# A chunked RWKV recurrence: level products on four quadrants of the array, rows of v from DRAM, outputs summed in PSUM

## The reference

```python
def wkv_scan(s0, r, w, k, v, a, b, reverse):
    def step(s, inp):
        r_t, w_t, k_t, v_t, a_t, b_t = inp
        sa = jnp.einsum('bhvk,bhk->bhv', s, a_t)
        s = s * w_t[:, :, None, :] + sa[..., :, None] * b_t[:, :, None, :] + v_t[..., :, None] * k_t[:, :, None, :]
        return s, jnp.einsum('bhvk,bhk->bhv', s, r_t)
```

## Time and profile before

| | us |
|---|---|
| median of 3 runs | 2601.62 |
| lowest, highest | 2598.08, 2608.76 |
| profiled execution | 2604.29 |
| its span in the profile | 2602.5 |
| TensorE busy in the span | 2314.5 (89%) |
| VectorE busy | 1688.6 (65%) |
| ScalarE busy | 1025.3 (39%) |
| GpSimd busy | 661.3 (25%) |

### The profile page before, as it was taken

How to read it: one execution, slowest core, us unless ns; L and a number is a source line. 1 busy time by engine, 2 the same in 40 slices (tenths; PEclk the granted TensorE clock), 3 DMA queues, 4 the chain that set the end, 5 groups by cost and what they waited for, 6 DMA issues and landing times. The chain is left out here.

```text
span 2602.5 us, 50127 instructions
## 1 busy us (share of the span) xinstructions
PE 2314.5 (89%) x20892; PEld 1847.3 (71%) x20892; DVE 1688.6 (65%) x2155; ACT 1025.3 (39%) x1633; POOL 661.3 (25%) x659
## 2 busy tenths in 40 slices
PE   5998988899999669999777999999973999999993
PEld 2886755568877558888636899997652888888883
DVE  5990559551115445666576776774657999999994
ACT  3112541231014420001154545444132877777773
POOL 1331568123320023222006666650000100000000
PEclk8998999999999779999878999998986999999997
DMA  6232004421104445211053111104142999999994
GB/s 237 96 124 75 1 33 142 132 99 45 49 14 185 151 156 193 96 41 40 14 185 92 32 32 29 29 20 169 57 174 97 409 407 396 396 393 405 396 378 158
DMA packets 136485, 401.77 MB, mean 154 GB/s; under 512 B 56314, under 2 KB 67834, under 8 KB 108754
## 3 DMA queue, kind: packets, MB, share of 16 engines
q1 hardware_dynamic: 124180, 360.02, 37.3%
q0 software_dynamic: 4608, 16.78, 2.7%
q10 hardware_dynamic: 7488, 21.99, 2.2%
HBM read 341.05 MB, written 57.69 MB: 153 GB/s over the span
## 5 line engine op out<-in xcount | busy, mean ns | idle before, releaser
L3900 DVE TENSOR_TENSOR ex_wl<-ew_raw,ex_wh 128x2048 fp32r<-128x2048 f32 x192 | 435.6, 2290 | 41.7 <-ACT ex_wh L3862 38.2
L3862 ACT ACTIVATE ex_wh<-ew_raw 128x2048 fp32r<-128x2048 f32 x192 | 367.6, 1919 | 109.5 <-PE ex_U L3806 40.3
L118 PE MATMUL sp_acc<-b2h_hi,sp_wh 128*128 128x512 f32 (+1 forms) x528 | 194.7, 369 | 16.2 <-POOL sp_wl L1729 16.2
L118 PE MATMUL sp_acc<-b2h_lo,sp_wh 128*128 128x512 f32 (+1 forms) x528 | 194.4, 368 | 0.0
L118 PE MATMUL sp_acc<-b2h_hi,sp_wl 128*128 128x512 f32 (+1 forms) x528 | 194.2, 368 | 0.0
L3783 POOL DMA_INDIRECT x<-ex_o,ex_at x16 | 26.5, 1656 | 490.2 <-DVE ex_o L3923 490.2
L2621 PE MATMUL rc_chain<-rc_x,rc_near 64*64 64x64 f32 x3200 | 132.8, 222 | 5.3 <-DVE rc_near L2503 2.2
L1727 POOL CAST sp_wh<-sp_w 128x1024 fp32r<-128x1024 f32 x26 | 28.3, 1088 | 402.2 <-DMA sp_w<-in_w_conv 221.4
L2621 PEld LDWEIGHTS rc_chain<-rc_x,rc_near 64*64 64x64 f32 x3200 | 111.1, 135 | 19.2 <-issue 9.0
L118 PEld LDWEIGHTS sp_acc<-b2h_hi,sp_wh 128*128 128x128 f32 x528 | 100.1, 190 | 33.9 <-POOL sp_wl L1729 16.6
L118 PEld LDWEIGHTS sp_acc<-b2h_lo,sp_wh 128*128 128x128 f32 x528 | 100.2, 190 | 16.4
(11 more groups left out here) (520 smaller groups left out, 5887.6 us busy)
## 6 DMA issues: line engine op xcount, KB each, us to landing
ew_raw<-in_exp_gate SPq DMA_DIRECT2D x64, 1024.0 KB, 8.0
ew_raw<-in_exp_up SPq DMA_DIRECT2D x64, 1024.0 KB, 9.5
ew_raw<-in_exp_down SPq DMA_DIRECT2D x64, 1024.0 KB, 8.0
b2p_pT<-in_ada_w SPq DMA_DIRECT2D x32, 512.0 KB, 6.0
rc_ac<-ac SPq DMA_DIRECT2D x40, 256.0 KB, 3.4
b_pj<-in_ada_w SPq DMA_DIRECT2D x8, 1024.0 KB, 12.5
ssm_wm<-in_w_merge SPq DMA_DIRECT2D x16, 512.0 KB
ac<-rp_ac SPq DMA_DIRECT2D x4, 2048.0 KB, 7.1
```

The lines of the kernel that those rows point to most:

```text
L118: ins = nc.tensor.matmul(out, w[a][:, k, :], h[b][:, k, cols], start=(first and n == 0), stop=(last and n == 2))
L3862: nc.scalar.activation(wh[:, n % RING], raw[:, n % RING], ACT.Copy).then_inc(q["w_hi"], 1)
L3900: V.tensor_tensor(wl[:, n % RING], raw[:, n % RING], wh[:, n % RING].bitcast(f32), ALU.subtract).then_inc(q["w_lo"], 1)
```

## The change

1. Level products: `diagonal` becomes `chain`. The second pair of blocks (j = 1) writes its result to the other half of the partitions (p ^ j), on the way back `advanced` takes it from there, so that the 8 matmuls go round all four quadrants. `chain` has one region in two banks for both products instead of one bank each.
2. For that, `advanced` needs the transposed matrix of the second pair of blocks in the other half: `moved` on ScalarE copies it into `xo`, two copies of 64 partitions by 128, at each of the five levels. `advanced` and `inverted` wait for `xt_moved`.
3. Rows of v: `rwkv_prepare` transposes v at its start on TensorE, ten tiles of 128 tokens; ScalarE copies them from PSUM (into `wide`, used later), and SP stores them in DRAM. `logits(0)` waits until all ten are copied. In the recurrence `load_v(c)` on SP fetches them straight into `uv` with eight transfers per chunk, after `s_done` and `y_crossed`. `v_staged` and both `v_rows` go.
4. Outputs: `outputs_of_state` goes. `outputs` makes, for each of four regions, four 64x64 matmuls with the state (start) and then four matmuls over 128 partitions (stop) into the same PSUM region; VectorE adds once to `y`.
5. The orders of all engines in the recurrence are written anew. Direction 1 now leads, and the context chunks and others run in a staggered way.

```diff
@@ rwkv_prepare: SP, ScalarE, TensorE
+                for i in range(TILES):
+                    sp.wait_ge(q["v_out"], i + 1)
+                    sp.dma_start(v_dram[i * P:(i + 1) * P, :], v_staged[:, i]).then_inc(q["v_stored"], 16)
...
+                for i in range(TILES):
+                    act.wait_ge(q["v_turned"], i + 1)
+                    nc.scalar.activation(v_staged[:, i], acc[:, i % 6 // 2, i % 2], ACT.Copy).then_inc(q["v_out"], 1)
...
+                for i in range(TILES):
+                    if i >= 6:
+                        pe.wait_ge(q["v_out"], i - 5)
+                    for b in range(HP):
+                        last = nc.tensor.transpose(acc[:, i % 6 // 2, i % 2, b * P:(b + 1) * P], pT[:, VB + b, i * P:(i + 1) * P], T.ident[:])
+                    last.then_inc(q["v_turned"], 1)
...
                     if u == 0:
+                        pe.wait_ge(q["v_out"], TILES)
@@ rwkv_chunks: SP
+                def load_v(c):
+                    for d in range(2):
+                        if c:
+                            sp.wait_ge(joint["s_done"], c)
+                        if c > CTX_CK:
+                            sp.wait_ge(joint["y_crossed"], c - CTX_CK)
+                        for e in range(2):
+                            own = t[d]["uv"][e * CK:(e + 1) * CK].rearrange("p f (j a) t -> p f j a t", a=2)
+                            rows = v_dram[at(c, d):at(c, d) + CK, :].rearrange("r (j a f t) -> r f j a t", a=2, f=2, t=CK)
+                            for f in range(2):
+                                sp.dma_start(own[:, f, :, 1 - e, :], rows[:, f, :, 1 - e, :]).then_inc(q[d]["v_loaded"], 16)
@@ ScalarE
-                        A.activation(t[d]["t1"][:], chained(d, 0), ACT.Copy).then_inc(q[d]["t1_ready"], 1)
+                        A.activation(paired(t[d]["t1"][:]), chained(d), ACT.Copy).then_inc(q[d]["t1_ready"], 1)
+
+                def moved(c, d, l):
+                    if runs(c):
+                        b, s = t[d], q[d]
+                        act.wait_ge(s["xt_next"], LEVELS * c + l + 1)
+                        for p in range(2):
+                            frm, to = slice(p * CK, (p + 1) * CK), slice((1 - p) * CK, (2 - p) * CK)
+                            A.activation(b["xo"][to], b["xt"][frm, 2:4], ACT.Copy).then_inc(s["xt_moved"], 1)
@@ VectorE
-                def outputs_of_state(c, d):
...
-                for k in range(NCK + 1):
+                for k in range(NCK + 2):
+                    advanced(k - 1, 0, 0)
+                    outputs(k - 2, 1)
...
@@ TensorE
-                def diagonal(d, bank, l, r):
...
+                def quarters():
+
+                    for f, j, p in product(range(2), range(HP // 2), range(2)):
+                        yield 2 * j + f, j, f, p, p ^ j
+
+                def chain(d, back, l, r):
+
+                    for h, j, f, p, o in quarters():
+                        frm, to = (o, p) if back else (p, o)
+                        k = slice(frm * CK, (frm + 1) * CK)
+                        last = M(chained(d)[to * CK:(to + 1) * CK, j, f], l(h, p)[k], r[k, h], start=True, stop=True)
...
+                        pe.wait_ge(s["xt_moved"], 2 * (LEVELS * c + l + 1))
+                        chain(d, True, lambda h, p: b["xo"][:, h - 2] if h >= 2 else b["xt"][:, h], b["t1"]).then_inc(s["xp_done"], 1)
...
-                        stacked(lambda b, f, j, e: (b["uv"][:, f, 2 * j + e], b["near"][:, c % 2, f, 1, 2 * j + e])).then_inc(joint["y_crossed"], 1)
...
+                        for j, d in product(range(HP // 2), range(2)):
+                            b, at = t[d], slice((2 * d + j) * CK, (2 * d + j + 1) * CK)
+                            for e, f in product(range(2), range(2)):
+                                k, h = slice(f * CK, (f + 1) * CK), 2 * j + e
+                                M(W[k, e, at], b["S"][k, h], b["ar"][k, c % 2, h, CK:], start=True, stop=False)
+                            for e, f in product(range(2), range(2)):
+                                k, h = slice(f * CK, (f + 1) * CK), 2 * j + e
+                                last = M(W[k, e, at], b["uv"][:, f, h], b["near"][:, c % 2, f, 1, h], start=False, stop=True)
+                        last.then_inc(joint["y_crossed"], 1)
```

272 lines of the change are left out of this document (120 added, 152 removed).

## The result

The changed kernel takes **2632.54 us** (median of 4 runs, 2631.96 to 2635.96); the kernel before took 2599.85 us beside it (2597.32 to 2608.76). The ratio is 1.0123, with a 95% interval of 1.0102 to 1.0143. The forecast was 2595.6 us with a range of 2555 to 2618: the direction was wrong and the range too low. The profiled execution has a span of 2630.3 us, against 2602.5 us before: 27.8 us more.

What follows compares the result with a forecast made beforehand. TensorE was taken to bound the recurrence. Prepare +7.0, context chunks -4.4, the 19.59 us chunk -1.5, 14 full chunks -8.1, last chunk and tail +1.0 gave -6.0 us; off the 2601.62 us median, 2595.6 us, range 2555 to 2618.

Steps and rivals of the forecast that it cites:

- The walk: Path followed through one recurrence chunk, engines strictly in order: 19.2 us against 19.78; 16.5 against 17.98 in context chunks.
- Level products on four quadrants: In the recurrence, 18 products per chunk go from 0.46 to 0.23 us, saving 4.1 us of TensorE per chunk.
- The rival that they don't run at once: Level products stay at 0.46 us in the recurrence: 20.4 us per chunk, 2618 us in all; chance 0.03.
- The outputs' block: On TensorE in the recurrence, 64 pairs with eight shape changes of 0.18 us last 3.2 us.
- `rwkv_prepare`: Phase ahead of the recurrence: first logits wait for ten copies of v and start 7.0 us later.
- The copies across: `moved` on ScalarE in the recurrence: 0.20 us a copy, 0.40 a pair, 0.54 until the product may start.
- the copies across cost more: Rival: a pair of `moved` copies takes 0.67 us, giving 20.3 us per chunk and 2615 us; chance 0.07.
- GpSimd's order has slack in it: In the chunk walk, GpSimd's last scaling of direction 0 is done at 16.6 us, when ScalarE is there too.
- the two lower rivals: TensorE stays close to the bound in the recurrence: 2575 us, or 2538 us if only its own work counts; chance 0.33.
- Rows of v: Loads in the recurrence: eighth issue at 13.4 to 13.9, wanted at 17.5, hidden below 3.6 to 4.1 us of landing.
- the rival of the late rows: Rows of v land late in the recurrence: 2615 us at 4.9 us of landing, 2655 at 7; chance 0.10.
- The clock: In the recurrence, TensorE was read at its full clock, 1.00, the 2.4 GHz level.

Runs made afterwards that it cites:

- e3_grouped: Changed kernel with the outputs' 64 pairs in two groups, first all products with the state, then all with u and v: 2617.84 us.
- e11_copies_twice: Changed kernel with each of the 20 `moved` copies per chunk made once more into a tile nobody reads: 2693.95 us.
- e1: Changed kernel without the 20 `moved` copies per chunk, products reading `xt` instead (inverse wrong for two of four heads): 2626.52 us.
- e7: Changed kernel with outputs summed in PSUM tile `own_half` instead of `crossing`, the state's half multiplied early: 2611.29 us.
- e12: e7 with the work of GpSimd, ScalarE, VectorE and TensorE in a new order: 2616.12 us, ratio to before 1.0068.
- e8_no_copies_slot_v: Changed kernel without `moved` copies, with a third slot for direction 1's scaled r, and rows of v loaded for the first chunk alone: 2625.96 us.
- e14_two_quad_v_stays: e13 with the rows of v loaded for the first chunk alone (wrong v afterwards): 2604.32 us.
- e13: Kernel before with only the rows of v from DRAM, two-quadrant products and orders made for it: 2616.43 us, ratio to before 1.0066.
- e16: Kernel before plus eight more 32 KB DRAM-to-DRAM DMAs behind each load of `ac` in the chunks, which nothing waits for: 2606.41 us.
- e4: Kernel before with only the rows of v from DRAM, in the old orders without the removed steps: 2690.24 us.

## Why the prediction was wrong, step by step

The walk gave 19.2 us for a full chunk and 20.6 is the regular one. Two of its steps failed: the pair of copies at 0.40 us, which takes 0.64, and GpSimd's slack, which isn't there. Three things were put at nothing and weigh something: the landing of the rows of v, the granted clock and the supply of instructions.

- **Level products on four quadrants: right.** 16 pairs pass in 0.22 to 0.23 us, where the earlier trace rows had 0.46. The rival that they don't run at once fell. The Trainium skill (TensorEngine Tiling (Array Packing), Restrictions and Gotchas) says that different row tiles can't use one PSUM bank at the same time. Here the trace differs: both row halves of these products write the same bank, in other partitions, at the full rate.
- **The outputs' block: right.** 3.07 us for 3.2 (eight loads 0.38 us apart, 0.22 and a shape change of 0.16). VectorE waits 2.68 us for it, as foretold. It stood on the path at two thirds of its price (e3_grouped).
- **TensorE's share: right**, 85% for 84%.
- **`rwkv_prepare`: right in kind.** The rows in order of time that answer to the earlier trace rows:

```profile
1285.27 5.00 ACT L1956 ACTIVATE rp_wide<-rp_acc 128x512 f32<-128x512 f32 x10 [3.71 <-DMA rp_restart<-in_restart]
...
1290.33 1.13 PE L2003 MATMUL rp_acc<-b2p_pT,rp_lora 64*128 64x512 f32 x4 [2.27 <-ACT rp_wide L1956]
```

  ScalarE begins at 1285.27, where 1285.3 was forecast, and needs 5.0 us for ten copies (5.9 forecast). The first logits start 6.1 us later than before, for 7.0; 4.0 us of it are left at the first `inverted`.
- **The copies across: the term was mis-sized.** The walk took 0.40 us for a pair and 0.54 until the product may start. The group in the trace after, from 1500 to 1700 (count, busy us, mean ns, idle before):

```profile
L2426 ACT ACTIVATE rc_xo<-rc_xt 64x128 f32<-64x128 f32 x190 | 58.5, 308 | 44.4 <-DVE rc_xt L2554 40.4
L2418 ACT ACTIVATE rc_t<-rc_chain 128x256 f32<-128x256 f32 x75 | 27.7, 370 | 1.5 <-PE rc_chain L2650 1.1
```

  A copy lasts 0.308 us, a pair 0.64, and the next instruction of ScalarE starts 0.54 to 0.62 after the pair. The upper bound of 0.67 was nearly the truth; a copy of half the partitions and half the columns costs four fifths of a whole one. By the prediction's own price (four pairs on the path, 1.1 us for 0.27 more each) 0.64 for 0.40 makes 1.0 us per chunk; the replay, again a calculation, gives 19.59 with 0.20 per copy and 20.19 with what was measured, 0.6 us. That they are on the path is shown by e11_copies_twice. The rival "the copies across cost more" had chance 0.07 and named 20.3 us.
- **"GpSimd's order has slack in it": wrong.** I had its last scaling of direction 0 at 16.6 us of the walk, "when ScalarE is there too". In the chunk shown it ends 17.6 us after `inverted`, and ScalarE waits 0.96 us for it. Even by my own number, `decay_out` at 16.7 and 2.9 us of ScalarE's work from there to `inverted` (1737.51 to 1740.43) make 19.6, not 19.2. I had put `inverted` behind `right_side`, and not behind the queue that the copies of g stand in.
- **TensorE's instructions: left out altogether.** This step is the one that no rival had. The walk counted the time of every product, at 14 ns a pair, and not how many pairs there are. In the kernel after itself the stops seen inside products are only 3.8 us in 340, 0.2 us per chunk. Those between two products can't be told from other waits one by one, but 15 more idle times, 8.6 us in all, end in the same window behind a packet. So it is 12.4 us in 340 at most, 0.8 per chunk. This cap takes part of what each other edit frees (e1, e7, e12), and the two lower rivals (2575 and 2538), with a third of the chances, came true in no order that was tried.
- **Rows of v: hidden by the list of waits only.** The prediction had `right_side` at 17.5 us of the walk and the eighth issue at 13.4 to 13.9. In the chunk shown the first issue starts at 10.6, the last rows land at 18.2 and `right_side` starts at 18.7. The eight issues take 5.5 us, where eight times 0.49 are 3.9. Another chunk, where the wait is plain (SyncE's queue, then the weight loads of `right_side`):

```profile
1668.06 6.09 SPq L2252 DMA_DIRECT2D rc_uv<-v_rows  x8
...
1676.84 0.59 PEld L2658 LDWEIGHTS rc_crossing<-rc_uv,rc_near 64*64 64x64 f32 x32 [0.72 <-issue]
```

  The last row lands at 1676.57. Nine of 19 chunks of the kernel after wait for v in this way, 2.7 us in all by their other waits (an estimate). So the rival of the late rows, with chance 0.10, was true in kind and small in size. With the 5 us of e8_no_copies_slot_v this part of the change, which I counted at -0.6 us of TensorE per chunk, gives little or nothing net: even e14_two_quad_v_stays, without the loads, is only 2.3 us shorter than before in the recurrence, with 5.4 us more of stops.
- **The clock: taken as full throughout.** The earlier trace rows had 1.00, and the walk then let TensorE idle 3 us per chunk at no further cost. In the kernel after it fell three times in the recurrence, each time after TensorE had waited more than before: some 5 us.

The sum against the forecast, in spans: prepare -3.0, context chunks +8.8 (19.4 for 16.5), the 14 full chunks +25.3 (21.0 for 19.2), the last interval +3.3 (20.45 for 16.16 + 1.0), the tail -0.5: together +33.9, which leads from -6.0 to +27.8 but for rounding. Of the 8.8 us of the context chunks 3.5 go with the lower clock. Of the 1.8 us per full chunk 1.4 are in all 14, as the 20.6 us of the regular ones: that is the loop with the copies at 0.64 us a pair and GpSimd's queue without slack. The six longer ones hold the other 5.6 us: 1.4 in the chunk with the lower clock, 3.7 in three chunks in which `right_side` waited for v (in the longest of them, 22.76 us, another wait ended only 0.08 us earlier). How the 1.4 us divide between the copies, GpSimd and stops at the borders of products stays open; the experiments show that copies and stops are there, not their share in this kernel, since they don't add up.

No kernel tried that leaves nothing out is faster than before. The nearest are e7_own_half and e12_new_order: they take back 19.4 and 19.8 of the 24.4 us in the recurrence, and their whole time is 5.7 us (one run) and 16.5 us (four runs) above before.

## What to carry to other kernels

Where a change makes small matrix products faster, count instructions and not only time: here 584 pairs per chunk at 124 pairs in 3.8 us have a floor near 17.9 us, and 19.4 at the middle distance of 4.1 us (estimates), and bursts above that pace are paid back as stops. When a part of the loop is moved from the busy engine to a chain of short steps, follow each queue to its last instruction before calling it slack; the wait that counted was that of a step that nobody on the path wanted, ahead of the one that was wanted. An edit that gives nothing when left out may still be on the path: double it as well, and compare stretches at the same granted clock. And an idle time that a list puts down to "issue" is not proof that nothing was waited for: hold its end against the landings of the transfers and the packets of instructions.

## What was not expected of the hardware

- TensorE's instructions arrive in packets of 16.4 KB, one for about 124 pairs of weight load and matmul in f32 (255 to 256 instructions). All 309 stops inside products end 1.16 to 1.63 us after such a packet; where two stops are one block apart, it is never less than 3.65 us. The stops last 0.15 to 1.6 us.
- With the rows of v loaded in each chunk the stops of the two-quadrant kernel are 14.7 us in 340, without 6.1 (e13, e14). Traffic that no instruction waits for brings 2.1 for 0.7 (e16, one run).
- A product starts 0.27 us after the last landing that it waited for, and the list of waits calls that "issue" (95 of 247 chunks).
- The granted clock fell to the 1.2 GHz level within the recurrence of every kernel in which TensorE waits much (after: three times 3.4 us; e4: 78 us of 456; e11: 109 of 455), and never in before, e13, e14 and e16.
- A ScalarE copy of 64x128 in SBUF from one half of the partitions to the other lasts 0.308 us, where one of 128x256 from PSUM lasts 0.370.
